# Two output stages of a streaming encoder step: softmax division moved to the heads, tile 0 by halves, loads and gating in another order

## The reference

```python
# layer 0: 8 heads of branch A and 8 of branch B; layer 1: 16 latent heads; 64 columns each
p = softmax(scores)                       # per head
o[:, head] = p @ v                        # 16 heads side by side: 1024 columns
mixed = o * silu(g)                       # gate rows, one per token
y = mixed @ w_out                         # 1024 x 1024
x = x + gate(c) * y                       # a gate per request
# layer 1 only: x = rms_norm(x, final_norm_g)
```

## Time and profile before

| | us |
|---|---|
| median of 3 runs | 1805.9 (1805.15 to 1806.75) |
| profiled execution | 1808.65, its span 1806.9 |
| PE busy | 1652.8 (91%) |
| DVE busy | 1275.9 (71%) |
| ACT busy | 945.3 (52%) |
| output stage of layer 0 | 929.7 to 1052 of the span |
| output stage of layer 1 | 1681.4 to the end |

### The profile page before, as it was taken

How to read it: one execution, slowest core, us unless ns; L and a number is a source line. 1 busy time by engine, 2 the same in 40 slices (tenths; PEclk the granted TensorE clock), 3 DMA queues, 4 the chain that set the end, 5 groups by cost and what they waited for, 6 DMA issues and landing times. The chain is left out here.

```text
span 1806.9 us, 34106 instructions
## 1 busy us (share of the span) xinstructions
PE 1652.8 (91%) x12719; PEld 1301.8 (72%) x12719; DVE 1275.9 (71%) x2739; ACT 945.3 (52%) x1916; POOL 304.3 (17%) x421
## 2 busy tenths in 40 slices
PE   4799799999999989999989989898959999999798
PEld 1566488888888867777767878687847676777687
DVE  2657489989887967888876557545438777777764
ACT  3535522246118267778862255365547677767421
POOL 4440100110000242322200000000033222320000
PEclk9799799999999999999989989999979999999899
DMA  9363324532334587877846433424241111111532
GB/s 355 90 206 126 89 75 118 152 111 88 81 101 140 183 190 218 252 193 196 243 131 225 175 135 101 108 67 121 67 108 46 30 29 38 29 29 45 182 132 94
DMA packets 188396, 230.31 MB, mean 127 GB/s; under 512 B 120213, under 2 KB 128501, under 8 KB 186186
## 3 DMA queue, kind: packets, MB, share of 16 engines
q1 hardware_dynamic: 168890, 169.94, 31.6%
q0 software_dynamic: 19344, 58.21, 10.6%
HBM read 170.25 MB, written 57.83 MB: 126 GB/s over the span
## 5 line engine op out<-in xcount | busy, mean ns | idle before, releaser
L685 PE MATMUL PS<-ab_wh,hT 128*128 128x512 f32 x576 | 229.7, 399 | 3.8 <-DVE ab_wl L1048 3.8
L686 PE MATMUL PS<-ab_wl,hT 128*128 128x512 f32 x576 | 227.3, 395 | 0.0
L687 PE MATMUL PS<-ab_wh,hT 128*128 128x512 f32 x576 | 226.0, 392 | 0.0
L1616 DVE TENSOR_SCALAR_CACHE_REDUCE topk_junk<-scores,topk_small 128x528 bf16<-128x528 f32 (+6 forms) x224 | 194.9, 916 | 1.3
L2822 DVE CUSTOM_DVE_ANT_0 la_S<-PS,la_mask 128x128 f32<-128x128 f32 (+3 forms) x144 | 107.6, 747 | 43.1 <-PE PS L687 29.9
L685 PEld LDWEIGHTS PS<-ab_wh,hT 128*128 128x128 f32 x576 | 108.6, 189 | 27.6 <-ACT ab_wh L977 3.9
L687 PEld LDWEIGHTS PS<-ab_wh,hT 128*128 128x128 f32 x576 | 108.4, 188 | 24.6
L686 PEld LDWEIGHTS PS<-ab_wl,hT 128*128 128x128 f32 x576 | 108.7, 189 | 22.7
L685 PE MATMUL PS<-out_wh,out_mT 128*128 128x512 f32 x288 | 116.3, 404 | 4.7 <-DVE out_mT L2299 4.7
L1994 ACT ACTIVATE at_P<-at_S,at_nm 128x128 f32<-128x128 f32 (+2 forms) x144 | 110.6, 768 | 11.5 <-DVE at_nm L2041 11.5
L2744 ACT ACTIVATE la_P<-la_S,la_nm 128x128 f32<-128x128 f32 (+3 forms) x144 | 110.3, 766 | 8.9 <-DVE la_nm L2822 8.6
(11 more groups left out here) (460 smaller groups left out, 4474.1 us busy)
## 6 DMA issues: line engine op xcount, KB each, us to landing
ab_wl_raw<-in_ab_w_in SPq DMA_DIRECT2D x64, 256.0 KB, 4.6
out_g<-scratch_gates_nat SPq DMA_DIRECT2D x18, 512.0 KB, 5.7
hT_raw<-in_ada_w SPq DMA_DIRECT2D x8, 1024.0 KB, 14.7
mod_w<-in_ada_w SPq DMA_DIRECT2D x16, 512.0 KB, 4.5
mod_w<-in_ada_w SPq DMA_DIRECT2D x8, 1024.0 KB, 5.4
ab_wl_raw<-in_cache_b_k POOLq DMA_DIRECT2D x8, 1024.0 KB, 7.5
ab_wh_raw<-in_cache_b_v POOLq DMA_DIRECT2D x8, 1024.0 KB, 11.7
scratch_qcT<-c_T SPq DMA_DIRECT2D x72, 96.0 KB, 2.1
```

What stands on the lines that cost most here:

```text
L685: nc.tensor.matmul(out, x[0], w[0], start=start, stop=False)
L686: nc.tensor.matmul(out, x[0], w[1], start=False, stop=False)
L687: return nc.tensor.matmul(out, x[1], w[0], start=False, stop=stop)
L1616: go(V.tensor_scalar(mark, x, limit, 0.0, op, ALU.add, accum_out=cnt[:, m:m + 1]), 0 if m == M - 1 else 1)
```

## The change

- **Division.** When the last of a head's results is in PSUM, DVE takes the reciprocal of that head's eight sums in place, waits for it, waits for `valued`, and multiplies bank 7 by it into `mix`, in both attention kernels. The reciprocal of all sums, `rinv` and the scaling in `gate_rows` go.
- **Tile 0 by halves.** Gating, transposes, high and low part of tile 0 run in two halves of 512 columns, each with its own count; `whole(i) = i + 2` is the count at which tile i is complete. PE's products of tile 0 wait for half 0, and from weight tile 4 on for half 1.
- **Order.** SP asks for gate rows 2 behind weight tile 5; the sample gates go behind gate rows 3 and have a semaphore of their own, waited for at tile 8. DVE gates tile 2 ahead of the low splits 6 and 7. PE transposes tile 1 after weight tile 3. ACT makes the high part of tile 1 ahead of the high splits 6 and 7.
- **Retirement.** Ahead of the output stage of layer 0 the list takes all store semaphores with four prefixes rather than the eight of the weights.

```diff
@@ attention (layer 0; layer 1 has the same with DV for DH)
                     if kind == "head" and i == QT - 1:
+                        dve.wait_ge(exped, it)
+                        nc.vector.reciprocal(c.sums[:, :, g:g + 1], c.sums[:, :, g:g + 1]).then_inc(weighed, 1)
+                        dve.wait_ge(weighed, g + 1)
                         dve.wait_ge(valued, tiles_done(g, i))
-                        nc.vector.tensor_copy(c.mix[:, :, g * DH:(g + 1) * DH], PS[:, 7, :].rearrange("p (i d) -> p i d", d=DH)).then_inc(resulted, 1)
+                        nc.vector.tensor_tensor(c.mix[:, :, g * DH:(g + 1) * DH], PS[:, 7, :].rearrange("p (i d) -> p i d", d=DH),
+                                                c.sums[:, :, g:g + 1].broadcast_to([P, QT, DH]), ALU.mult).then_inc(resulted, 1)
@@ mixed_out
+        whole = lambda i: i + 2
@@ sync
                 if i >= 2:
-                    sp.wait_ge(gated, i - 1)
+                    sp.wait_ge(gated, whole(i - 2))
...
                 if k == 3:
                     load_gates(1)
+                if k == 5:
+                    load_gates(2)
             load_x(0)
             sp.dma_start(gate[:], dram(c.s["gate"], l * NR * D, [[0, P], [1, D]])).then_inc(rows_in, 16)
-            sp.dma_start(sample_gate[:], dram(c.s["gate"], (l * NR + 1) * D, [[D, NB], [0, TS], [1, D]])).then_inc(rows_in, 16)
             if last_layer:
                 sp.dma_start(fg[:], dram(c.i["final_norm_g"], 0, [[0, P], [1, D]])).then_inc(rows_in, 16)
-            load_gates(2)
             load_x(1)
             load_gates(3)
+            sp.dma_start(sample_gate[:], dram(c.s["gate"], (l * NR + 1) * D, [[D, NB], [0, TS], [1, D]])).then_inc(sample_in, 16)
@@ tensor
             def turn(i):
-                if i < QT:
-                    pe.wait_ge(gated, i + 1)
-                else:
+                if i >= QT:
                     pe.wait_ge(g_in[i % 2], 16 * (i // 2 + 1))
                 if i >= 2:
-                    pe.wait_ge(mT_lo, i - 1)
+                    pe.wait_ge(mT_lo, whole(i - 2))
                 src = c.mix[:, i, :] if i < QT else g(i)
                 for k in range(KT):
+                    if i < QT and k % 4 == 0 and (i == 0 or k == 0):
+                        pe.wait_ge(gated, whole(i) if k or i else 1)
+                    if i == 0 and k == 4:
+                        last.then_inc(tr_done, 1)
...
             turn(0)
-            pe.wait_ge(mT_lo, 1)
             for k in range(KT):
+                pe.wait_ge(mT_lo, 1 + k // 4)
                 pe.wait_ge(w_lo, k + 1)
...
-                if k == 5:
+                if k == 3:
                     turn(1)
@@ scalar
             def high(i):
+                if i == 0:
+                    for a in range(2):
+                        act.wait_ge(tr_done, a + 1)
+                        nc.scalar.activation(mT[:, 0, 0, 4 * a:4 * a + 4, :].rearrange("p a b -> p (a b)"), PS[:, a, :], ACT.Copy).then_inc(mT_hi, 1)
+                    return
...
-            for k in range(3):
+            for k in range(2):
                 split_high(k)
             high(0)
-            for k in range(3, KT):
+            for k in range(2, KT):
+                if k == 6:
+                    high(1)
                 split_high(k)
-            high(1)
@@ vector
             def gate_rows(i):
-                mv = c.mix[:, i, :].rearrange("p (h d) -> p h d", d=DH)
-                chain(nc.vector.tensor_tensor(mv, mv, rinv[:, i, :].unsqueeze(2).broadcast_to([P, HC, DH]), ALU.mult))
                 dve.wait_ge(g_in[i % 2], 16 * (i // 2 + 1))
-                nc.vector.tensor_tensor(c.mix[:, i, :], c.mix[:, i, :], g(i), ALU.mult).then_inc(gated, 1)
+                for cols in HALVES if i == 0 else [slice(0, D)]:
+                    nc.vector.tensor_tensor(c.mix[:, i, cols], c.mix[:, i, cols], g(i)[:, cols], ALU.mult).then_inc(gated, 1)
+
+            def low_half(a):
+                dve.wait_ge(mT_hi, a + 1)
+                hi, lo = (mT[:, 0, d, 4 * a:4 * a + 4, :].rearrange("p a b -> p (a b)") for d in range(2))
+                nc.vector.tensor_tensor(lo, PS[:, a, :], hi, ALU.subtract).then_inc(mT_lo, 1)
...
-            chain(nc.vector.reciprocal(rinv[:], c.sums[:]))
             gate_rows(0)
-            for k in range(2):
-                split_low(k)
-            low(0)
+            split_low(0)
+            low_half(0)
+            split_low(1)
+            low_half(1)
             for k in range(2, 4):
                 split_low(k)
             gate_rows(1)
-            for k in range(4, KT):
+            for k in range(4, 6):
+                split_low(k)
+            gate_rows(2)
+            for k in range(6, KT):
                 split_low(k)
             low(1)
-            gate_rows(2)
-            dve.wait_ge(rows_in, 32 + 16 * last_layer)
+            dve.wait_ge(rows_in, 16 + 16 * last_layer)
...
             i = NT - 1
+            dve.wait_ge(sample_in, 16)
@@ build, ahead of layer 0's output stage
-            IN_USE.extend(weights.w_in)
+            IN_USE.extend(STORES[n] for n in STORE_NAMES if n.startswith(("ix_", "cum_", "ab_", "first_")))
             retire_semaphores(nc)
```

More of the change, by code:

```diff
@@ L1720, in branches_ab @@
     emask_done, cleared, built, v_hi, v_lo, causal = S("emask"), S("cleared"), S("built"), S("v_hi"), S("v_lo"), S("causal")
-    scored, maxed, exped, turned, high, valued, resulted, inverted = (
-        S(n) for n in ("scored", "maxed", "exped", "turned", "high", "valued", "resulted", "inverted"))
+    scored, maxed, exped, turned, high, valued, resulted, inverted, weighed = (
+        S(n) for n in ("scored", "maxed", "exped", "turned", "high", "valued", "resulted", "inverted", "weighed"))
     unit_free = [S(f"unit_free{n}") for n in range(3)]
@@ L2215, in _ @@
                     turn(i + 1)
-                pe.wait_ge(mT_lo, i + 1)
+                pe.wait_ge(mT_lo, whole(i))
                 if i >= 2:
@@ L2292, in low @@
                 else:
[L2293 removed]
+                    dve.wait_ge(tr_done, whole(i))
                     for a in range(2):
```

15 lines of the change are left out of this document (9 added, 6 removed).

## The result

The changed kernel takes 1792.23 us (median of six runs, 1789.60 to 1797.77), the kernel before 1806.33 beside it (six runs, 1804.45 to 1811.13): a ratio of 0.9932, 95% interval 0.9915 to 0.9948. That is 12.3 us less by the ratio (9.4 to 15.4). 1791.2 was forecast, with a gain of 14.7. The profiled execution of the changed kernel took 1790.64, its span 1788.8.

A forecast was written before the change was run, and what follows sets the result against it. TensorE, busy 91% of the span, was taken as the bound, with time lost at the output stages' starts. Gains of 7.3 and 7.4 us, charges included, make 14.7: median 1805.9 to 1791.2 us, range 1787.5 to 1798.

The forecast's parts named there:

- the sum: Whole kernel: gains of 7.3 us in layer 0's output stage and 7.4 in layer 1's, 14.7 with both charges taken.
- Front of the stage: Output stage start: without reciprocal and scaling, and by halves, layer 0's first product at 933.5 instead of 937.6 us.
- Weights as the path to the end of tile 0: Output stages: the last weight tiles, landing 1.28 us later, set tile 0's end at 947.5 and 1699.25 us.
- rival 1: Output stages: half clock stays longer or tile 0's residual comes late; gain only 7 to 11 us; chance 0.25.
- Tile 2 without a hole: Output stages: tile 2 gated before its use, transposes follow tile 0's end, the next tile's 11.86 us later.
- What is late next: Tile 0's residual, waiting for broadcasts: layer 1's tile 3 gated 0.9 us before wanted, capping that layer's gain at 8.3.
- the equal price of 3.1 us for each broadcast: Load queue in layer 1's output stage: each of three broadcasts priced at 3.1 us, putting the residual's start at 1702.3.
- Clearing: Semaphore retirement ahead of layer 0's output stage: two more pairs of drain and clear, +0.5 us (0 to 1.0).
- Heads: Attention heads: multiply for copy costs nothing, reciprocal with wait about 0.25 us, hidden except layer 1's last head.
- Rival 2: Attention heads pay: 0.94 us a head, 30 us over 32, on VectorE's path, giving 1821 us; chance 0.05.
- Rival 3: Output stages: what is won at one hole is waited at the next; within 3 us of before; chance 0.05.

The follow-up runs named there:

- tile0_whole: The change, but with gating, high and low part of tile 0 each done whole instead of by halves: 1795.12 us, ratio to the kernel before 0.9948.
- recip_early: The change, but with each head's reciprocal moved ahead of the score maximum of the same step, away from the multiply: 1793.62 us in one run.
- kept_busy: The change plus eleven transposes of the identity, results unread, in TensorE's two holes at the start of an output stage: 1787.23 us in one run.
- best: The change with eleven unread transposes added, tile 1's high part after all splits, and only neighbouring semaphores cleared: 1787.33 us, ratio to the kernel before 0.9914.

## Why the prediction was right, and where it was off

The time, 1791.2 against 1792.23, and the place of the gain were right. That the time fits so closely is in part luck: the sum had 14.7 where the account has 12.7, and misses within it offset each other. Point by point:

- **Front of the stage: right.** The first product 3.27 and 3.26 us after the release; worked out were 3.3 (933.5 less 930.2).
- **Weights as the path to the end of tile 0: not in the change; the time was right in layer 1, 1.5 us short in layer 0.** Worked out were 17.3 and 17.55 us from the release to tile 2's transposes (947.5 less 930.24; 1699.25 less 1681.70, as the last head moves the release by 0.25). Measured 18.77 and 17.56. In layer 0 the step that failed is the arrival of the last weight tile as the bound: the half clock lasted 5.5 us of products instead of 3.4, so tile 1's transposes came at 11.48, ACT's high part of tile 1 behind them, and the last two high splits, queued behind that, ended 15.5 us after the release rather than 14.5. The products of the last two weight tiles, one tile after the other behind the wait of 0.65 us, made 0.5 more than the six products of the sum. The forecast had ACT's new order in its sum for layer 1 alone. There the turned tile 1 was to be done 12.65 us after the release (1694.1 less 1681.45) and was at 12.37; the last high split ended 0.5 sooner than worked out, its low part with it, and the same products of two tiles took the 0.5 back: 17.56 is two misses that offset. That the path runs through the first product and PE, and not through the loads, is what tile0_whole shows. The run with the high part behind the splits and the run with PE kept busy bring layer 0 to 29.5 or less at tile 3, where 29.2 was forecast; the second profile of the change has 29.97 without either. This is near rival 1 in its first half, at 0.8 to 1.4 us in one layer, though the clock rose some 2.3 us sooner after the release than before.
- **Tile 2 without a hole, 11.86 a tile, no second fall of the clock: right** (11.81, 1.00).
- **What is late next: the mechanism right, the size off.** The residual of tile 0 in layer 1 was to start 20.6 us after the release and leave 0.9 us of margin. It started at 17.8, tile 3's gating was over at 1696.66 and wanted at 1700.28: 3.6 us. The failed step is the equal price of 3.1 us for each broadcast: by their landings 5.4 us were lost behind the sample gates, and 2.0 (with an instruction load in it) and 1.3 went for the two others; the dear one had been moved out of the way. In the changed kernel the norm row lands (1688.5) just as tile 0's products end (1688.64).
- **Clearing: right in size,** 0.42 for two more pairs against 0.5.
- **Heads: exchange free, right; wholly hidden, not quite.** Copy and multiply take 692 ns both. The reciprocal took 0.20 and the last head of layer 1 pays 0.24 (0.25 forecast): the reciprocal at 1669.68, the multiply at 1669.92, without a gap to the copies before. But the idle time ahead of the multiply went from 5.2 to 4.6 in layer 1, and not by the 3.1 us that sixteen reciprocals take, and some 0.7 us beyond the last head's share is paid there. The step that failed is that the idle time ahead of the multiply covers all that the division adds; recip_early shows that the cost stays when the reciprocal is elsewhere, and the cause is open. In layer 0 the idle time fell by 2.5; what was paid there is lost in the spread of 259.5 to 264.9 us.
- **Rival 2** (heads cost 0.94 us each) is ruled out: 304.2 against 303.3 us for layer 1's heads, and in layer 0 a spread of 5 us where 15 would have been paid. **Rival 3** didn't occur in the change, but it is what each part does without the new order.

The Trainium skill's section "Part 1: The HAM clock gate (the "warmup" mystery)" in "TensorE: Matmul & The Clock Gate", named in the prediction, has activity release the clock; kept_busy agrees (1.00 in layer 1 where the change had 0.56). There it bought nothing at tile 3, as the last weight tile landed 0.7 us later than in the change.

The gain of the sum, 14.7, against 12.7 by the account: 1.4 lies in layer 0's tile 0 (0.8 by the second profile), 0.7 in the heads of layer 1.

## What to carry to other kernels

When a stage starts with several waits in a row, work out for each what is late next, down to the load that ends it: here division and halves brought the first product 4.6 us forward, and the kernel stayed slower than before as long as the queue asked for tile 2's rows no sooner. A hole that gets longer can cost more than its length, since the clock may fall behind it (3.93 us of hole, 14.7 us instead of 11.8 for the tile after); the length alone doesn't tell, as before the change the clock fell behind 2.03 us in layer 0 and not behind 2.50 in layer 1. Price transfers one by one: a mean over three hid one that held the queue up about four times as long as the cheapest. And take the same kernel's profile twice before a difference of half a microsecond is given a cause.

## What was not expected of the hardware

- A transfer that spreads one row of 4 KB over all 128 partitions took 1.3 us in the queue, what a plain load of the same 512 KB takes (1.28). One that spreads eight rows over sixteen partitions each held the row behind it back by 5.4 us, at about 200 GB/s with all DMA engines busy instead of about 400.
- A load of 16 KB of instructions made the 512 KB transfer under way beside it land 0.7 to 1.3 us later, weight tile 7 in four runs and the gate in four others.
- The clearing of semaphores cost about 0.17 us for each short run of neighbouring numbers.
- Eleven transposes without use, in two holes of 2.3 and 1.2 us, kept TensorE's clock at 1.00 through the start of layer 1, in kept_busy and in best alike.
- The division in layer 1's heads cost 0.7 us beyond the last one's share, wherever in the step its reciprocal of 0.20 us stood and though the multiply takes what the copy took. Why is open.
